# Prompt attention: the order of the eight row tiles in a round of heads

## The reference

```python
(q, kc, vc, ksl, vsl, kw, vw, gts, hc, bc, cc, z), gate = modulate_project(xp, c_prompt, ...)
o_attn = nsa_prompt(q, gts, kc, vc, ksl, vsl, kw, vw, cmpw, rel_bias)
u = cc * hc
y_conv = bc * short_conv(pad(u), conv_w)
xp = merge_output(xp, gate, o_attn, y_conv, z, w_out)
```

## Time and profile before

| what | value |
|---|---|
| median of 3 runs | 1485.69 us |
| the profiled execution's own time | 1483.41 us |
| its span | 1481.6 us |
| TensorE busy | 1421.1 us |
| VectorE busy | 960.5 us |
| ScalarE busy | 704.1 us |
| mean granted TensorE clock | 0.991 |

### The profile page before, as it was taken

The page is one execution under the profiler, slowest core; times in us unless marked ns, Lnnn a source line. Parts: engine busy times, 40 slices in busy tenths (PEclk is TensorE's granted clock), DMA queues, the critical chain, the costliest instruction groups (busy, mean ns, idle before and its releaser), DMA issues.

```text
span 1481.6 us, 27910 instructions
## 1 busy us (share of the span) xinstructions
PE 1421.1 (96%) x10526; PEld 1225.8 (83%) x10526; DVE 960.5 (65%) x2309; ACT 704.1 (48%) x1546; POOL 236.2 (16%) x447
## 2 busy tenths in 40 slices
PE   4999999999999999989989989989999999999998
PEld 1889999999999999977767777777777766788886
DVE  2646878878787787767776576576666554643226
ACT  2332233332322323256677777777777756621111
POOL 1201020110101101131021242232231141000000
PEclk9899999999999999999999999999999999999999
DMA  9335733332333323597121321121121039963321
GB/s 343 109 107 113 123 116 87 93 92 61 108 80 93 104 49 108 133 338 247 60 94 32 74 73 44 45 78 44 39 58 30 22 112 346 279 205 100 90 85 36
DMA packets 169861, 164.76 MB, mean 111 GB/s; under 512 B 53756, under 2 KB 150268, under 8 KB 164352
## 3 DMA queue, kind: packets, MB, share of 16 engines
q1 hardware_dynamic: 153904, 94.11, 23.3%
q0 software_dynamic: 15824, 68.87, 15.2%
HBM read 131.27 MB, written 35.83 MB: 113 GB/s over the span
## 4 chain that ended last, share of the span: by engine, by line
PE 88%; DVE 4%; DMA 4%; ACT 2%; issue 2%; SPq 1%; POOL 0%; DVEq 0%; ACTq 0%
PE PS L1269 34%; PE PS L1636 12%; PE PS L1442 8%; PE PS L1407 7%; PE PS L1386 5%; PE PS L1387 4%; PE PS L1321 3%; PE PS L1226 2%; PE PS L1227 2%; PE PS L1228 2%; DMA adaw<-in_ada_w 1%; DMA kwb<-in_cache_k_win 1%; PE PS L1593 1%; PE PS L1433 1%; PE PS L1489 1%
## 5 line engine op out<-in xcount | busy, mean ns | idle before, releaser
L1269 PEld LDWEIGHTS PS<-bo,wsl 128*128 128x128 f32 x4104 | 499.4, 188 | 0.4 <-issue 0.4
L1269 PE MATMUL PS<-bo,wsl 128*128 128x264 f32 x4104 | 499.6, 284 | 0.0
L1897 ACT ACTIVATE pr<-PS,nm 128x640 f32<-128x640 f32 (+7 forms) x256 | 181.1, 709 | 44.6 <-DVE nm L2399 42.0
L1732 ACT ACTIVATE wsl<-wsum 128x512 fp32r<-128x512 f32 x105 | 65.6, 631 | 237.8 <-DVE wsum L2122 237.8
L1920 ACT ACTIVATE ptt<-PS 128x512 f32<-128x512 f32 x264 | 149.6, 601 | 43.1 <-PE PS L1407 42.9
L1407 PE MATMUL PS<-ident,pr 128*128 128x128 f32 x1056 | 147.2, 274 | 0.3 <-ACT ptt L1920 0.3
L1442 PE MATMUL PS<-ptt,kvt 128*64 128x256 f32 x1056 | 136.7, 390 | 0.0
L1407 PEld LDWEIGHTS PS<-ident,pr 128*128 128x128 f32 x1056 | 122.4, 141 | 9.2 <-issue 0.6
L1442 PEld LDWEIGHTS PS<-ptt,kvt 128*64 128x64 f32 x1056 | 66.9, 136 | 41.2 <-issue 16.5
L2399 DVE CUSTOM_DVE_ANT_0 PS<-PS,near,nm 128x256 f32<-128x256 f32 x192 | 94.7, 493 | 6.8
L2398 DVE TENSOR_REDUCE nm<-PS 128x1 f32<-128x128 f32 (+5 forms) x128 | 70.5, 551 | 39.6 <-PE PS L1387 38.9
(11 more groups left out here) (358 smaller groups left out, 2371.1 us busy)
## 6 DMA issues: line engine op xcount, KB each, us to landing
wr<-in_w_in SPq DMA_DIRECT2D x32, 512.0 KB, 5.5
adaw<-in_ada_w SPq DMA_DIRECT2D x8, 1024.0 KB, 10.0
wr<-in_w_in SPq DMA_DIRECT2D x32, 256.0 KB, 4.5
q_stacked<-qp POOLq DMA_DIRECT2D x64, 128.0 KB, 2.7
qb<-q_stacked SPq DMA_DIRECT2D x32, 256.0 KB, 3.1
mr<-mixed SPq DMA_DIRECT2D x16, 512.0 KB, 3.8
mixed<-yy POOLq DMA_DIRECT2D x16, 264.0 KB
xb<-in_x_prompt POOLq DMA_DIRECT2D x8, 512.0 KB, 4.3
```

Of the source, the lines that this page charges most:

```text
L1269: ins = pe.matmul(PS[:, 2 * q + c, 0:H // 2], w[:, x, kk, :], b[:, y, kk, c * H // 2:(c + 1) * H // 2], start=(first and kk == 0 and x == ...
L1897: act.activation(pr[r][:, h, 0:k], score_cols(b0, w), ACT.Exp, scale=-1.0, bias=nm[:, r, h:h + 1], accum_out=rsum[:, r, h:h + 1]).then_inc ...
```

## The change

One line. The round of eight row tiles rose over the even tiles and fell over the odd ones; now tile 0 stands next to 7, 1 next to 6, and so on. All that is derived from `unit(u)` follows: the bank of each head, the loads and the stores.

```diff
 NPT5 = 8
-TILE_ORDER = (0, 2, 4, 6, 7, 5, 3, 1)
+TILE_ORDER = (0, 7, 1, 6, 2, 5, 3, 4)
 NWE = 7
```

## The result

The changed kernel takes 1523.63 us in the median of 6 runs (1521.25 to 1528.41), the kernel before 1486.68 us (1485.40 to 1490.59). The ratio is 1.0251, with a 95% interval of 1.0239 to 1.0263: slower by 37 us. The forecast was 1514 in a range of 1498 to 1538. The profiled execution took 1523.61 us for a span of 1521.8.

What follows compares the result with a forecast made beforehand. The Tensor engine was taken to bound the kernel. A round of 60.6 + 62.2 = 122.8 us against 115.6 gives +7.2, four make +29: 1483.41 becomes 1512, with 2.3 to the median 1514 us, range 1498 to 1538.

Steps and rivals of the forecast that it cites:

- W: Tensor engine's work in prompt-attention step i→j (tile i turned, j scored): 0.905 n(i) + 0.47 n(j) + 2.34 us, n key tiles.
- 7→1: Step turning tile 7 while scoring tile 1: Tensor engine always busy, put at 16.0 us.
- The loop of long-next steps: Steps scoring tiles 4 to 7: third two-bank head waits for the first's exponentials; together 62.2 us a round.
- The excess over W and C: Added over the larger of W and C: 1.2 (0→7), 1.6 (1→6), 2.2 (2→5), 1.9 us (3→4).
- C: Least time of a step scoring tile 4, 5, 6, 7, from its heads' bank round trips: 12.2, 13.0, 13.6, 14.4 us.
- Short-next steps: Steps 7→1, 6→2, 5→3 and 4→0: cost the Tensor engine's work, together 60.4 us a round, plus 0.2.
- The ends: Attention's tail: last unit tile 4, not 1, adds 5.4 us; one missing 4→0 step, 5.5 more, cancels it.
- rival (c): Granted clock falls in 0→7 and 1→6, 2.26 us each: +18 on the forecast, 1532 us; chance 0.16.
- (a): Averaging: only engine totals count, every attention round shrinks to 109.5 us, time falls by 24 to 1461; chance 0.07.
- (b): The bank loop counts but the excess over it vanishes: no change, 1486 us; chance 0.06.
- (d): Hand-over between one-bank and two-bank heads adds 2 us per long-next step: +32 on the forecast, 1546 us; chance 0.08.
- SyncE's tables: Sample-stage tables, 29.9 us at the fifth unit ahead of its store: hidden by 7 us, costing nothing.

Runs made afterwards that it cites:

- the descending order: Kernel before, with the unit order (0, 7, 6, 5, 4, 3, 2, 1) in each round: 1496.94 us, ratio 1.0069.
- the tables moved: Kernel before with unit order (0, 7, 6, 5, 4, 3, 2, 1) and SyncE's sample tables issued at the ninth unit, not the fifth: 1489.07 us, ratio 1.0018.
- Taking VectorE's far part out: Changed kernel without VectorE's reduction or edge mask over keys more than 256 back: 1493.85 us, ratio 1.0044.
- the run without the far part: Kernel before without VectorE's reduction or edge mask over keys more than 256 back: 1471.21 us, ratio 0.9896.
- the early release: Changed kernel, with value products in windowed halves released from two transposed tiles on, not four: 1516.41 us, ratio 1.0199.

## Why the prediction was right, and where its size was off

- **TensorE's work W.** 7→1 was put at 16.0 and took 16.05. The formula, fitted to three steps, also gives 7→7 (20.2, measured 20.18) and 6→5 (18.4, measured 18.41 in the descending order). It held for these. It does not hold between short units, where carried products count: with the tables moved, 2→1 took 8.4 for a W of 9.6 and 1→0 took 8.1 for 6.9.
- **The loop of long-next steps.** 0→7, 1→6, 2→5 and 3→4 were put at 15.6, 15.2, 15.2 and 16.2; measured 15.31, 15.23, 15.11 and 16.03, together 61.7 for 62.2. Taking VectorE's far part out showed that the head's round trip is in what sets them. The excess over W and C was not derived, only carried over from the old order, and for 3→4 that was in part luck: its 1.9 stood between 2→4 and 4→6, and the 1.5 of 4→6 is mostly no stall. TensorE was busy for 18.24 of the 18.53 us there, and line 1442 has 48 records for tile 4's 40, 0.94 us carried from 2→4:

```profile
883.64:902.17 18.53, 6.06 (x48) 3.09 (x48) 1.00 0.15 43
```

- **0→2, left without a cause.** The largest of the old stalls, 2.5 us, has one-bank heads on the scoring side. The prediction counted it in the 6.1 us and explained only 2→4 and 4→6; the run without the far part shows that VectorE is in it (9.37 to 7.99 us). The forecast needed only that it goes.
- **Short-next steps: the mis-sized term.** "Together 60.4, plus 0.2" came out as 13.09 + 16.05 + 16.46 + 16.95 = 62.55, 1.9 us a round more. Carried products are 1.3 to 1.4 of it (the early release gave back 0.43 and 0.88 us): I charged a unit's values to its own step, but 0.47 and 0.94 us of them run in 6→2 and 5→3. That does not shorten 1→6 and 2→5, which the loop holds anyway. 4→0 was 0.8 over. Its 128-key score matmuls start 0.15 and 0.11 us apart (lines below), where a price per column has 0.06, but that can be only about half of it: 1→0 of the kernel before scores the same tile, and took 6.84 for 6.9 with 12 records of value products for tile 1's 16, 0.47 us less, so it stood 0.4 over. The other 0.4 of 4→0 is open.

```profile
982.55 0.31 PE L1386 MATMUL PS<-ksh,qb 128*128 128x128 f32 x1
982.70 0.28 PE L1387 MATMUL PS<-ksl,qb 128*128 128x128 f32 x1
982.81 0.63 PE L1407 MATMUL PS<-ident,pr 128*128 128x128 f32 x4
```

- **The sum.** 124.2 us a round for 122.8, 8.7 more than before where I had 7.2. The ends cancelled as foretold: 5.8 us more in the tail, one 4→0 less. The first round did not behave as the others: without its 4→0 the forecast leaves it 1.7 us, and it grew by 5.3. The old 0→2 took only 7.65 us there, 1.9 less than in round 2, and the first unit's step took 7.86 for 6.36. With rounds 2 to 4 (27.1 for 21.6), the tail (5.8 for 5.4) and the start (1.2 sooner) that makes the 37.0 for 28.7. Of the 9.6 us by which 1514 fell short, 8.3 lie here; 1.0 is the median of the kernel before, 1486.68 with all runs for 1485.69.
- **The clock, rival (c).** Falls came in 6→2 of round 2 (18.09 for 16.46) and 0→7 of round 4 (16.91 for 15.31), some 1.6 us each, against one of 2.3 before. A third, in 0→7 of round 1 (0.89), did not lengthen the step (15.21 us). Nothing near the +18 of the rival.
- **Rivals (a), (b), (d).** Averaging is out, as the rounds grew; the excess over W and C stayed; and steps did not exceed the forecast by a hand-over.
- **SyncE's tables.** In the changed order line 2439 never waits for the store, as worked out. The price of that rival is shown by the descending order, 8 us.

## What to carry to other kernels

In a pipeline that looks one unit ahead, cost each step as the larger of the bottleneck's own work and the round trip of the next unit's buffers, and expect some excess where a step is held by the round trip (0.9 to 2.2 us here); a long unit next to a short one loses the work that hid its round trip. Long units belong beside long ones, and units of many rounds can be sorted together: here 1.0% faster with every instruction kept. Before moving units, look for one-off queue bursts tied to a unit's number and for work that is carried over a unit's end.

## What was not expected of the hardware

The granted clock fell with no wait of TensorE over 3.3 us in the attention: 6→2 of round 2 ran at 0.91 with TensorE busy throughout, after a 1→6 step in which it was busy 12 of 15.2 us. In the descending order with late tables 0→7 ran at 0.90 in rounds 2 and 4 and at 1.00 in round 3, with the same tiles before it each time. What tells these apart stays open.
